# Block two's attention front re-ordered: rope in halves, four-head items, later copies of weights

## The reference

```python
def hybrid_layer(x, mod, ...):
    h = rms_norm(x, norm1) * (1.0 + scale1) + shift1
    proj = h @ w_in                    # u (512), q (512), k and v (6 x 128), gates (24)
    y_pool = pool_mixer(u, pool_w, pool_scale)
    y_nsa = nsa_mixer(q, k, v, gates, q_norm, k_norm, cmp_pe, cmp_w1, cmp_w2)
    x = x + gate1 * (jnp.concatenate([y_pool, y_nsa], -1) @ w_out)
    h2 = rms_norm(x, norm2) * (1.0 + scale2) + shift2
    return x + gate2 * (jnp.square(jax.nn.relu(h2 @ w_ff1)) @ w_ff2)

def nsa_mixer(...):                    # 8 heads of 64, 2 key groups
    q = rope(rms_norm(q, q_norm), pos)
    k_s, k_w = (rope(rms_norm(k[i], k_norm[i]), pos) for i in (1, 2))
    k_cmp, v_cmp = compress(k[0], ...), compress(v[0], ...)   # 31 blocks, a two-layer net
    k_cmp = rope(rms_norm(k_cmp, k_norm[0]), cmp_end)
    o_cmp = softmax(mask(q @ k_cmp.T)) @ v_cmp
    # of 8 blocks of 64 keys up to 16 are selected, and the window is 512: both are all causal keys
    o_s, o_w = causal softmax attention of q on k_s, v_s and on k_w, v_w
    return g[0] * o_cmp + g[1] * o_s + g[2] * o_w
```

## Time and profile before

| | us |
|---|---|
| median of three runs | 2769.2 (2763.6 to 2769.5) |
| the profiled execution | 2767.8 |
| its span | 2766.0 |
| TensorE busy | 2514.3 (91%) |
| VectorE busy | 1373.0 (50%) |
| ScalarE busy | 953.3 (34%) |
| GpSimd busy | 875.1 (32%) |

### The profile page before, as it was taken

The page is one execution under the profiler, slowest core; times in us unless marked ns, Lnnn a source line. Parts: engine busy times, 40 slices in busy tenths (PEclk is TensorE's granted clock), DMA queues, the critical chain, the costliest instruction groups (busy, mean ns, idle before and its releaser), DMA issues.

```text
span 2766.0 us, 34344 instructions
## 1 busy us (share of the span) xinstructions
PE 2514.3 (91%) x12303; PEld 2003.8 (72%) x12303; DVE 1373.0 (50%) x3041; ACT 953.3 (34%) x1707; POOL 875.1 (32%) x366
## 2 busy tenths in 40 slices
PE   7998989899999899989978778999998777899999
PEld 6676877678867687767876447888887644788887
DVE  4587233654467733365364554354465554523235
ACT  4432243432443234342343452322224354332221
POOL 4242413234423242323332002454542200244442
PEclk9999999999999999999998799999999888999999
DMA  5132414135422242313432002444433200233332
GB/s 181 54 91 77 152 39 130 50 97 181 143 61 69 92 145 62 107 54 122 147 102 65 1 1 61 145 155 149 161 121 86 65 1 1 62 95 104 99 100 77
DMA packets 132174, 256.02 MB, mean 93 GB/s; under 512 B 21914, under 2 KB 28588, under 8 KB 132012
## 3 DMA queue, kind: packets, MB, share of 16 engines
q1 hardware_dynamic: 132012, 253.83, 29.3%
HBM read 249.60 MB, written 4.19 MB: 92 GB/s over the span
## 4 chain that ended last, share of the span: by engine, by line
PE 74%; DVE 16%; ACT 5%; issue 3%; DMA 1%; SPq 0%; ACTq 0%; DVEq 0%
PE ps L752 60%; PE ps L706 4%; DVE arena L1685 2%; DVE top L1683 2%; PE ps L1041 1%; PE ps L899 1%; PE ps L1002 1%; PE ps L814 1%; PE ps L879 1%; DMA raw<-in_w_out_dram 1%; DMA raw<-in_w_in_dram 1%; PE ps L874 1%; DVE ps L1625 1%; DVE nsm L1399 1%; DVE soft L1960 1%
## 5 line engine op out<-in xcount | busy, mean ns | idle before, releaser
L682 POOL TENSOR_TENSOR wl<-raw,wh 128x1024 fp32r<-128x1024 f32 (+2 forms) x362 | 874.9, 2423 | 1862.5 <-ACT wh L1062 1861.6
L752 PE MATMUL ps<-wh,hTh 128*128 128x512 f32 (+3 forms) x1600 | 645.1, 403 | 1.1 <-DVE hTl L1629 1.1
L1062 ACT ACTIVATE wh<-raw 128x1024 fp32r<-128x1024 f32 (+2 forms) x362 | 379.1, 1049 | 745.5 <-PE ps L752 364.1
L752 PE MATMUL ps<-wh,hTl 128*128 128x512 f32 (+3 forms) x1600 | 624.7, 390 | 0.0
L752 PE MATMUL ps<-wl,hTh 128*128 128x512 f32 (+3 forms) x1600 | 624.6, 390 | 0.0
L752 PEld LDWEIGHTS ps<-wh,hTh 128*128 128x128 f32 x1600 | 310.9, 194 | 76.8 <-issue 19.5
L752 PEld LDWEIGHTS ps<-wh,hTl 128*128 128x128 f32 x1600 | 309.5, 193 | 60.3
L752 PEld LDWEIGHTS ps<-wl,hTh 128*128 128x128 f32 x1600 | 310.9, 194 | 52.1
L752 PE MATMUL ps<-hTh,wh 128*128 128x512 f32 (+2 forms) x704 | 259.0, 368 | 3.8 <-DVE hTl L1629 2.3
L752 PE MATMUL ps<-hTh,wl 128*128 128x512 f32 (+2 forms) x704 | 257.8, 366 | 0.0
L752 PE MATMUL ps<-hTl,wh 128*128 128x512 f32 (+2 forms) x704 | 257.7, 366 | 0.0
(11 more groups left out here) (266 smaller groups left out, 3229.8 us busy)
## 6 DMA issues: line engine op xcount, KB each, us to landing
raw<-in_w_in_dram SPq DMA_DIRECT2D x160, 512.0 KB, 3.6
raw<-in_w_ff_dram SPq DMA_DIRECT2D x128, 512.0 KB, 3.6
modw<-in_w_mod_dram SPq DMA_DIRECT2D x96, 512.0 KB, 4.7
raw<-in_w_br_dram SPq DMA_DIRECT2D x24, 512.0 KB, 3.7
raw<-in_w_out_dram SPq DMA_DIRECT2D x24, 512.0 KB, 3.6
xm<-in_x_dram SPq DMA_DIRECT2D x8, 512.0 KB, 4.2
raw<-in_w_out_dram SPq DMA_DIRECT2D x16, 256.0 KB, 3.8
raw<-in_w_in_dram SPq DMA_DIRECT2D x8, 408.0 KB, 3.2
```

What stands on the lines that cost most here:

```text
L682: pool.tensor_tensor(piece(wl, g % RING, u), piece(raw, g % RING, u), piece(wh, g % SPLIT, u).bitcast(F32), ALU.subtract)\
L752: last = pe.matmul(*args, start=(q == 0 and c == 0 and n_pass == 0), stop=(q == u["quarters"] - 1 and c == u["chunks"] - 1 and n_pass == 2))
L1062: act.activation(piece(wh, g % SPLIT, u), piece(raw, g % RING, u), ACT.Copy)\
```

## The change

It has five parts. (1) `rstd ek` and `rstd eq` are each issued twice, for two tiles at a time. (2) `k_rope` and `q_rope` are split into a rotation (`k_rot`, `q_rot`, VectorE) and the turn with its copy, and all are placed earlier; the compression's network moves from `eu` into `eq`. (3) Tiles 0 and 1 have items of four heads (`MANY`), 24 items in a layer; the scaling of such an item is one TENSOR_TENSOR with the scales broadcast. Tile 0 gets buffers of its own (`PP0`) and PSUM banks 2 and 3 (`logit0`), while `eu` accumulates in banks 0 and 1 (`low`). (4) Tile 0's four items stand between pairs of `eu`'s sweeps; gate row, bands and pools move to later items, and four sweeps of `mix0` stand beside the last four steps of the pipeline. (5) In the whole program ScalarE issues the copies that a sweep made possible at the next sweep's place.

```diff
+MANY = [2, 2, 1, 1]
+QUADS = [(t, j, p) for t in range(TILES) for j in range(2) for p in range(0, 4, MANY[t])]
...
-            norm_head(("a", l), U("ek", E_K, 384, tok(384), w="w_in_2", act=("a", l)), [("layer", l)])
-            line.append(("rstd", l, "ek"))
+            norm_head(("a", l), U("ek", E_K, 384, tok(384), w="w_in_2", act=("a", l)), [("layer", l), ("rstd", l, "ek", 0)])
             ev = U("ev", E_V, N_V, tok(N_V), w="w_in_2", act=("a", l))
-            weave([[], [], [], []] + [[("k_rope", l, t)] for t in range(TILES)], ev)
             eq = U("eq", E_Q, 512, tok(), w="w_in_2", act=("a", l))
-            cmp = [[("cmp_turn", l, t)] for t in range(TILES)] + [[("cmp_in", l, 0)], [("cmp_in", l, 1)]]
-            weave(cmp, eq)
-            line.append(("rstd", l, "eq"))
-            late = [[("cmp_hidden", l, 0)], [("cmp_hidden", l, 1), ("q_rope", l, 0)], [("cmp_key", l)], [("cmp_value", l), ("q_rope", l, 1)],
-                    [], [("cmp_key_turn", l), ("q_rope", l, 2)], [], [("q_rope", l, 3)]]
-            weave(late, U("eu", E_U, 512, tok(), w="w_in_2", act=("a", l)))
-
-            items = [(t, j, p) for t in range(TILES) for j in range(2) for p in range(4)]
+            eu = U("eu", E_U, 512, tok(), w="w_in_2", act=("a", l))
+            line[-4:] = line[-4:-3] + [("k_rot", l, 0), ("k_rot", l, 1)] + line[-3:]
+            weave([[("rstd", l, "ek", 1), ("k_rot", l, 2)], [("k_rope", l, 0)], [("k_rope", l, 1)], [("k_rot", l, 3)], [],
+                   [("k_rope", l, 2), ("cmp_turn", l, 0)], [("k_rope", l, 3), ("cmp_turn", l, 1)], []], ev)
+            weave([[], [("cmp_turn", l, 2)], [("cmp_turn", l, 3), ("cmp_in", l, 0), ("cmp_in", l, 1)], [],
+                   [("rstd", l, "eq", 0), ("cmp_hidden", l, 0), ("cmp_hidden", l, 1), ("q_rot", l, 0)], [],
+                   [("cmp_key", l), ("cmp_value", l)], [("q_rope", l, 0), ("q_rot", l, 1)]], eq)
+            items = QUADS
             def at_unit(name, n):
                 return [(name, l, *items[n])] if 0 <= n < len(items) else []
 
-            for n in range(-1, len(items) + 4):
-                t, j, p = items[n] if 0 <= n < len(items) else (0, 2, 0)
-                if n == -1:
-                    line.append(("cmp_logits", l, 0))
-                line.extend(at_unit("pair_turn", n - 2) + at_unit("pair_logits", n + 1))
-                if n >= 3 and n - 3 < len(items) and items[n - 3][2] == 3:
+            first = lambda n: at_unit("pair_logits", n) + at_unit("pair_max", n) + at_unit("pair_exp", n) + at_unit("pair_prob", n)
+            first = lambda n: at_unit("pair_logits", n) + at_unit("pair_max", n) + at_unit("pair_exp", n) + at_unit("pair_prob", n)
+            line.extend([("rstd", l, "eq", 1)] + first(0) + [("q_rot", l, 2)] + eu[0:2] + [("q_rope", l, 1)])
+            line.extend(at_unit("pair_turn", 0) + first(1) + [("q_rot", l, 3)] + eu[2:4] + [("q_rope", l, 2)])
+            line.extend(at_unit("pair_turn", 1) + first(2) + eu[4:6] + [("cmp_key_turn", l), ("q_rope", l, 3)])
+            line.extend(at_unit("pair_turn", 2) + first(3) + [("cmp_logits", l, 0), ("cmp_prob", l, 0)] + eu[6:8])
+            line.extend(at_unit("pair_turn", 3) + at_unit("pair_logits", 4) + [("cmp_turn2", l, 0)])
+            beside = {}
+            for t, n in enumerate((4, 8, 14)):
+                beside[n] = [("cmp_logits", l, t + 1)]
+                beside[n + 1] = [("cmp_prob", l, t + 1)]
+                beside[n + 2] = [("cmp_turn2", l, t + 1)]
+            for g, n in enumerate((5, 7, 11, 17)):
+                beside.setdefault(n, []).append(("pool_band", l, g))
+                beside.setdefault(n + (3 if g == 0 else 2), []).append(("pool", l, g))
+            beside[22] = [("gate_row", l, 0)]
+            mix = U("mix0", 0, 512, tok(), w="w_out_2", act="mix") + U("mix1", 512, 512, tok(), w="w_out_2", act="mix")
+            for n in range(4, len(items) + 4):
+                line.extend((at_unit("pair_turn", n - 2) if n >= 6 else []) + at_unit("pair_logits", n + 1))
+                if n >= 3 and n - 3 < len(items) and items[n - 3][2] + MANY[items[n - 3][0]] == 4:
                     line.append(("pair_value", l, *items[n - 3][0:2]))
-                if n >= 4 and items[n - 4][1:] == (1, 3):
+                if n >= 4 and items[n - 4][1] == 1 and items[n - 4][2] + MANY[items[n - 4][0]] == 4:
                     line.append(("o_split", l, items[n - 4][0]))
-                line.extend(at_unit("pair_max", n) + at_unit("pair_exp", n) + at_unit("pair_prob", n - 1))
-                if n == 0:
-                    line.append(("cmp_prob", l, 0))
-                if n == 1:
-                    line.append(("cmp_turn2", l, 0))
-                if n == 3:
-                    line.append(("gate_row", l, 0))
-                if (j, p) == (0, 2):
-                    line.append(("pool_band", l, t))
-                if (j, p) == (1, 0):
-                    line.append(("pool", l, t))
-                if (j, p) == (1, 1) and t + 1 < TILES:
-                    line.append(("cmp_logits", l, t + 1))
-                if (j, p) == (1, 2) and t + 1 < TILES:
-                    line.append(("cmp_prob", l, t + 1))
-                if (j, p) == (1, 3) and t + 1 < TILES:
-                    line.append(("cmp_turn2", l, t + 1))
-            line.extend(U("mix0", 0, 512, tok(), w="w_out_2", act="mix") + U("mix1", 512, 512, tok(), w="w_out_2", act="mix"))
+                line.extend(at_unit("pair_max", n) + at_unit("pair_exp", n) + (at_unit("pair_prob", n - 1) if n >= 5 else []))
+                line.extend(beside.get(n, []))
+                if n >= len(items):
+                    line.append(mix.pop(0))
+            line.extend(mix)
...
+                        bank("low" if u["name"] == "eu" else "proj", ("ps", i, s))
...
-                    while made[0] < min(unread[step] + SPLIT, G):
+                    while made[0] < min(unread[seen_sweep[0]] + SPLIT, G):
                         high(made[0])
                         made[0] += 1
+                    seen_sweep[0] = step
...
-                        ins = act.activation(PP[:, n % 2, o, 0:W], ps[:, b0 + o, 0:W], ACT.Exp, bias=s[:, 2 + o:3 + o],
-                                             scale=0.125, accum_out=s[:, 4 + o:5 + o])
+                        for i in range(MANY[t]):
+                            x, w = MANY[t] * o + i, slice(i * W, (i + 1) * W)
+                            ins = act.activation(prob_of(t, n)[:, o, w], ps[:, b0 + o, w], ACT.Exp, bias=s[:, k + x:k + x + 1],
+                                                 scale=0.125, accum_out=s[:, 2 * k + x:2 * k + x + 1])
...
+                        nh, half = {"ek": 8, "eq": 16}[name], step[3]
+                        s, v = stat[:, SS[name], nh * half:nh * half + nh], nsm[:, 0, 0:nh]
+                        dve.wait_ge(dve_result, at("sumsq", l, name, 2 * half + 1))
...
+                    if m == 2:
+                        quad = lambda x: x.rearrange("p (o i) -> p o i", o=2)
+                        dve.tensor_tensor(quad(s[:, 0:4]), quad(s[:, 12:16]), part.rearrange("p (i o) -> p o i", o=2), ALU.mult)\
+                            .then_inc(dve_result, mark(dve_result))
+                        dve.wait_ge(dve_result, now(dve_result))
+                        x4 = prob_of(t, n)[:, :, 0:2 * W].rearrange("p o (i w) -> p o i w", i=2)
+                        dve.tensor_tensor(x4, x4, quad(s[:, 0:4]).unsqueeze(3).to_broadcast([P, 2, 2, W]), ALU.mult)\
+                            .then_inc(dve_result, mark(dve_result, ("prob", l, n)))
```

More of the change, by code:

```diff
@@ L364, in build @@
             keys = [("scr", step)]
-        elif step[0] in ("k_rope", "q_rope", "cmp_key"):
+        elif step[0] in ("k_rot", "q_rot", "cmp_key"):
             keys = [("scr", step)]
@@ L1063, in high @@
                     .then_inc(act_high, mark(act_high, ("high", g)))
-            made = [0]
+            made, seen_sweep = [0], [next(x for x in line if x[0] == "sweep")]
             def scratch(key):
@@ L1829, in _ @@
                         dve.wait_ge(dve_result, now(dve_result))
-                elif kind in ("k_rope", "q_rope"):
+                elif kind in ("k_rot", "q_rot"):
                     _, l, t = step
                     key = ("scr", step)
-                    name, nh = ("ek", 4) if kind == "k_rope" else ("eq", 8)
+                    name, nh = ("ek", 4) if kind == "k_rot" else ("eq", 8)
                     x = (ktk if name == "ek" else qtk)[:, t, 0:64 * nh]
@@ L1937, in _ @@
                     b0 = bank_of.get(step, 0)
+                    if t == 0:
+                        dve.wait_ge(product, at("turned", ("q_rope", l, TILES - 1)))
+                        dve.memset(tokr[:, :, :], 0.0).then_inc(dve_result, mark(dve_result, ("PTc_cleared", l)))
                     dve.wait_ge(product, at("cmp_logits", l, t))
```

99 lines of the change are left out of this document (57 added, 42 removed).

## The result

| | before | after |
|---|---|---|
| median | 2769.1 us | 2693.5 us |
| runs | 2763.6 to 2769.5 (4) | 2690.7 to 2695.4 (4) |
| span of the profiled execution | 2766.0 | 2693.6 |
| TensorE busy / idle in it | 2514.3 / 251.7 | 2487.0 / 206.6 |
| mean granted clock | 0.954 | 0.964 |

The ratio of the times is 0.9731, 95% interval 0.9714 to 0.9747. The change is faster by 75.6 us where the prediction said 41.6. Of the 72.4 us by which the span fell, 45.1 are idle time of TensorE and 27.3 are shorter matmuls.

A forecast was written before the change was run, and what follows sets the result against it. TensorE, busy 91%, bounds the kernel; its waits in block two also lower its clock. Terms of -0.9 + 14.7 + 3 + 4 = 20.8 us a layer, 41.6 in two, took 2767.8 to 2726.2 us; range 2690 to 2760.

The forecast's parts named there:

- the forecast's own: Whole program: the prediction's main case, its terms' sum of 2726 us with range 2712 to 2740, chance 0.44.
- rival A: Block two: late copies move GpSimd's subtractions so they lock nothing out; 34.8 us a layer, 2698 us, chance 0.20.
- the prediction's own signs: Right: 6 to 9 us waits at `k_rope 0` and tile 0's first turn, clock over 0.85; wrong: block one changed over 8.
- the late weight copies: Whole program, ScalarE's copies one sweep later: 0, bounds -8 and +6 us, as TensorE waits for neither copy nor subtraction.
- Keys: Block two, key ropes by halves: a 7.6 us wait at `k_rope 0` against 4.16 + 2.59 before; -0.9 us a layer.
- Queries and tile 0: Block two, query ropes and tile 0's attention: waits of 12.7 us for 19.1, 7.6 at the first turn; +6.4 a layer.
- The clock: Block two, windows at clock 0.76 and 0.65: at most 12.3 us lost, 4 of it left; +8.3 us a layer.
- Tile 1: Block two, tile 1's attention in four-head items: +3 us a layer, between a ceiling of +7 and -3.
- The end: Block two, four mix0 sweeps beside a layer's last items fill TensorE's idle time: +4 us a layer, bounds 1 and 4.2.
- Gate row, bands, pools: Block two, work only moved to later items, filling waits of tiles 1 to 3: 0 us.
- B: Block two: TensorE's clock stays low and tile 1 gains nothing; 9.5 us a layer, 2749 us, chance 0.23.
- D: Block two's fronts: VectorE becomes the bound, its operations stalled by subtractions; slower, 2784 us, chance 0.08.

The follow-up runs named there:

- no_subtract: Changed kernel with the low parts of ev's four weight pieces and eq's first set to zeros instead of subtracted on GpSimd (left out of the result): 2676.3 us.
- tile1_pairs: Changed kernel with tile 1 in items of two heads instead of four, its neighbours shifted by four items: 2707.9 us.
- behind_evac: Kernel before, with weight copies at their own sweep's place but behind the evacuations of that sweep's product instead of ahead: 2769.6 us, ratio 0.9996.
- two_late: Changed kernel with ScalarE's weight copies issued two sweeps late instead of one: 2706.9 us.

## Why the prediction was right, and where not

**The time** came 33 us lower than predicted. Measured 2693.5 for 2726, in a range of 2690 to 2760 near its lower end, and below the forecast's own 2712 to 2740. That it lies inside is partly luck: the range's lower edge came from rival A, whose mechanism did not happen, and the term that was missing is in none of the cases. By the prediction's own signs the waits at `k_rope 0` and at the first item were right, as was the clock in the stretch of `eu` (0.92 for "over 0.85"), and block one, 23.5 us shorter where more than 8 was to count as wrong, was not.

**The step that failed** is the late weight copies, put at 0 with bounds of -8 and +6 over the program. They are worth 20 us on the kernel before (22 in block one, less the loss in block two) and 50 on the changed one. The step argued that TensorE waits for neither copy nor subtraction. That is so, but it asked who waits for the copy and not what stands behind it on ScalarE, where the copy must wait for its sweep and for its load. Its other argument, that a subtraction moved by one sweep can fall on or off a chain, was right in kind: it was bounded at -8 and +6 us, and one wait of block one alone, behind the masks, fell by 5.1 us over the two layers.

**Keys.** The wait of 7.6 came as worked out, 7.63; the first half of `rstd` took 10.0 us from its start, where the sum had 10.8 from tile 1's sum. `no_subtract` put the price of the lock at 8.6 us a layer, where rival A had 7.6 at this place.

**Queries and tile 0.** The wait at the first item's turn, 7.6 by the sum, came as 7.2 and 7.0 in layers one and two, partly by luck. VectorE's queue, taken as 16.9 us, lasted 20.7 (2109.18 to 2129.91): the key chain took 9.1 and not 5.2, with two of its operations under subtractions. But it began 1.9 us ahead of `eq`'s last sweep, and TensorE needed 11.9 us from that sweep to the turn, not 9.3. `q_rope 0` did not wait, for 2.4 taken, and `q_rope 1` waited 0.3, not 1.9; the first logits waited 1.2, which the sum lacked.

**Layer two, wait by wait** (those over 0.3 us): -0.9 at the keys as forecast; 9.8 for 6.4 at queries and tile 0; 1.5 for 3 in tile 1; 3.0 in tiles 2 and 3, whose moved neighbours had been put at 0; 1.8 for 4 at the end. That is 15.2 for 12.5, and idle time fell by 15.3.

**The clock.** Its +8.3 a layer was right only with late copies: matmul time fell by 4.8 and 11.7 us in the two layers with them, and by -0.4 and 1.7 without them, where the layers kept 0.90 and 0.89. Without late copies idle time fell by 12.4 and 11.5, just the 12.5 of the sum's waits. So the kernel that the sum really described would have gained 12 to 13 us a layer, not 20.8. That two errors met there, a clock that needs the late copies and a price of 0 for them, kept the layers' sum near the measured 22.5 and 27.0.

**Tile 1** was mis-sized: `tile1_pairs` has 7 for 3, most of it matmul time in layer two and not waits. **The end**: 2 for 4. **Gate row, bands, pools** were not tried alone.

**The rivals.** A's number, 2698, is the nearest, but its mechanism did not happen: the subtractions stayed where they were and locked VectorE in full. B's low clock is nearly what the change has without its late copies: 0.78 in the stretch of `eu`, for 0.92 with them and 0.7 as B's sign. D did not come; VectorE's share is 52%.

Open: how block one's 22 us divide between head of line and moved subtractions, and how much of them is the clock that came with shorter waits. TensorE's idle time there fell by 11 us (1342 - 1230.5 to 1318.5 - 1218.1) and its busy time by 12.5. Open too is why the late copies shorten block two's matmuls in the new order and lengthen them in the old one, by 15 and 9 us in one execution each; it is the larger part of what the two parts of the change do together, and no run tried it.

## What to carry to other kernels

An operation that waits costs what stands behind it on its engine, not only what waits for it: look at the idle time that the profile puts before a group even where that engine is far from busy. But take it as a place to look, not as a price: 92 us less of it gained nothing in `behind_evac`, and another 150 less came with a loss in `two_late`, since what such an operation triggers (here subtractions) moves too. Before a change of order is put down to one engine's queue, follow the wait back to the operation that ended it. Price the parts of a change together: parts 1 to 4 were worth 26 us with the copies in their old place and 56 with late ones, most of the difference in matmul time. When a wait is the sum of a queue on one engine, moving the waiter or the order of the queue only moved the wait here; taking work out of the queue paid.
